# Attention of a hybrid encoder trunk: V becomes the stationary operand, the transposed probabilities move, and two heads share the array's column halves

## What is computed

```python
# A: chunks of 64 queries see their own chunk and the 8 before it
s = jnp.einsum('bnqhd,bnkhd->bnhqk', qc, kb) * (dh ** -0.5)
p = jax.nn.softmax(s + bias, axis=-1)
o = jnp.einsum('bnhqk,bnkhd->bnqhd', p, vb)
oa = o * jax.nn.silu(az)
# C: the same over the 256 best keys of an indexer
p = jax.nn.softmax(jnp.where(sel_ok, s, -jnp.inf), axis=-1)
oc = jnp.einsum('bhqk,bqkhd->bqhd', p, vsel) * jax.nn.silu(cz)
# later: y = sigmoid(ga) * (oa @ w_branch[0]) + ... + sigmoid(gd) * (od @ w_branch[3])
```

## Time and profile before

| | us |
|---|---|
| median of 3 runs (3464.01 to 3467.62) | 3464.07 |
| the profiled execution | 3473.63 |
| its span | 3471.6 |
| TensorE busy in the span | 3128.5 (90%) |
| VectorE, ScalarE, GpSimd busy | 1799.1, 816.6, 668.0 |
| attention C, first layer | about 564 to 692 of the span |
| attention A, first layer | about 1384 to 1511 |
| attention C and A, second layer | about 2284 to 2412, 3103 to 3228 |

### The profile page before, as it was taken

The page is one execution under the profiler, slowest core; times in us unless marked ns, Lnnn a source line. Parts: engine busy times, 40 slices in busy tenths (PEclk is TensorE's granted clock), DMA queues, the critical chain, the costliest instruction groups (busy, mean ns, idle before and its releaser), DMA issues. The chain is left out here.

```text
span 3471.6 us, 45936 instructions
## 1 busy us (share of the span) xinstructions
PE 3128.5 (90%) x18504; PEld 1679.5 (48%) x18504; DVE 1799.1 (52%) x3456; ACT 816.6 (24%) x1542; POOL 668.0 (19%) x476
## 2 busy tenths in 40 slices
PE   7999996899998988899988999968999988898997
PEld 3444443545764446554443534435457544466443
DVE  2179996273334780245112799954722358702542
ACT  2141122431112422410110412234311123324000
POOL 1016331021112313000010163310311122130000
PEclk9999998989999999889999999988999989998998
DMA  5001121010011122054040011200110110210621
GB/s 197 13 15 37 58 79 43 10 42 29 23 41 50 34 69 73 4 183 130 0 140 15 25 37 52 94 25 16 34 47 17 38 49 29 85 54 4 231 81 55
DMA packets 132346, 195.77 MB, mean 56 GB/s; under 512 B 8072, under 2 KB 87976, under 8 KB 131880
## 3 DMA queue, kind: packets, MB, share of 16 engines
q1 hardware_dynamic: 113544, 158.74, 14.1%
q10 hardware_dynamic: 18592, 34.09, 2.7%
HBM read 146.14 MB, written 48.78 MB: 56 GB/s over the span
## 5 line engine op out<-in xcount | busy, mean ns | idle before, releaser
L504 PE MATMUL ps<-hT,wr 128*128 128x512 f32 x1600 | 759.3, 615 | 12.0 <-ACT arena L559 9.2
L504 PEld LDWEIGHTS ps<-hT,wr 128*128 128x128 f32 x1600 | 299.7, 196 | 343.3 <-issue 320.9
L504 PE MATMUL ps<-sums,wr 128*128 128x512 f32 x800 | 395.2, 626 | 13.9 <-ACT gts L569 13.9
L1314 DVE TENSOR_SCALAR_CACHE_REDUCE arena<-arena,sm 128x384 f32<-128x384 f32 (+5 forms) x384 | 337.9, 943 | 2.2
L649 POOL TENSOR_TENSOR gts<-gts,wr 128x512 f32<-128x512 f32 x96 | 132.6, 1381 | 749.7 <-ACT wr L550 494.6
L1032 DVE CUSTOM_DVE_ANT_0 arena<-ps,arena 128x640 f32<-128x640 f32 (+7 forms) x128 | 90.6, 708 | 310.2 <-PE ps L959 249.6
L504 PEld LDWEIGHTS ps<-sums,wr 128*128 128x128 f32 x800 | 151.5, 199 | 178.2 <-issue 155.8
L727 PE MATMUL ps<-xo,arena 128*128 128x512 f32 x512 | 224.0, 600 | 0.9 <-ACT xo L902 0.9
L739 PE MATMUL ps<-wr,hT 128*128 128x512 f32 x512 | 220.1, 592 | 0.0
L504 PE MATMUL ps<-wr 128*128 128x512 f32 x400 | 193.5, 612 | 2.9 <-ACT wr L550 2.9
L989 PEld LDWEIGHTS ps<-arena 128*128 128x128 f32 x1056 | 154.9, 218 | 79.4 <-issue 72.9
(11 more groups left out here) (293 smaller groups left out, 4475.8 us busy)
## 6 DMA issues: line engine op xcount, KB each, us to landing
wr<-in_w_in SPq DMA_DIRECT2D x68, 1024.0 KB, 5.3
gate_tanh<-gts ACTq DMA_DIRECT2D x128, 256.0 KB, 2.0
arena<-gate_tanh SPq DMA_DIRECT2D x128, 256.0 KB, 3.1
x_cur<-arena SPq DMA_DIRECT2D x2, 4096.0 KB, 23.4
arena<-in_w_branch SPq DMA_DIRECT2D x8, 1024.0 KB, 6.5
wr<-in_w_out SPq DMA_DIRECT2D x8, 1024.0 KB, 7.6
arena<-x_cur SPq DMA_DIRECT2D x4, 2048.0 KB, 8.1
arena<-in_x SPq DMA_DIRECT2D x4, 1024.0 KB, 8.1
```

The source lines that it names most:

```text
L504: ins = pe.matmul(ap, lhsT=right(u, w_side)[:, kt, :], rhs=left(h_side, kt), start=fresh and kt == 0, stop=kt == half_k - 1, skip_group_ch ...
L1314: ins = dve.tensor_scalar(compared[i], iscore[i], cbits[:, j:j + 1], None, ALU.is_ge, ALU.add, accum_out=count[:, j:j + 1])
```

## The change

For the values, V is now the stationary operand (128 keys x 64 channels) and the transposed probabilities move (128 columns). The result is transposed already: channels on partitions, queries in columns. Two heads go to the two column halves of the array, that is to partitions 0 to 63 and 64 to 127 of `O`, and are done together at every odd step from `u = 3` on. Even steps hold no values any more. The probabilities get a third buffer. The gate rows `z` are scaled by the reciprocals of the row sums on VectorE (at `u % 4 == 0`), transposed on TensorE in place of the gated output (at `u % 4 == 1`), copied by ScalarE into `xo` as before, and VectorE multiplies them there by `O` (at `u % 4 == 2`). The loop has 34 steps in place of 36, so two steps' fills are done elsewhere. The tail waits for `O` to be emptied where it waited for the ScalarE copy (two lines, in `pe_tail` and `sp_tail`).

```diff
@@ -715,7 +715,7 @@
             pe_fill(pe, KT * len(fills))
             assert fill_at[0] == len(fills) and len(piece_of) == 64 and not todo
-            jobs.stored(pe, ("oT", ORDER[-1], NT - 1))
+            jobs.stored(pe, ("o", ORDER[-1], NT - 1))
             for n, (half, ct, b) in enumerate(tail):
                 key = ("branch", n)
                 if n == 0:
@@ -921,12 +921,12 @@
         MIX = {}
-        def attention(b, q, k, v, z, first_tile, bias, at_s, at_pt, at_og, v_unit=None):
+        def attention(b, q, k, v, z, first_tile, bias, at_s, at_pt, v_unit=None):
             units = [(i, h) for i in range(NT) for h in range(4)]
             rows = [H(at_s), H(at_s + 1)]
-            probs_t = [H(at_pt), H(at_pt + 1)]
-            gated = [H(at_og, 0.25), H(at_og + 0.25, 0.25)]
+            probs_t = [H(a) for a in at_pt]
+            out_t = xo[:, 2 * ORDER.index(b):2 * ORDER.index(b) + 2, :]
             top, neg, tot, rtot = small(2), small(2), small(8), small(8)
             def span(u):
@@ -944,10 +944,10 @@
                 i, h, _, _ = span(u)
                 act_fills(eng, ("values", b, u))
-                if h == 3:
+                if h >= 2:
                     jobs.ready(eng, ("o", b, i))
                 else:
-                    eng.wait_ge(sg("values_" + b), 3 * i + h + 1)
+                    eng.wait_ge(sg("values_" + b), i + 1)
             def scores(pe, u):
@@ -970,39 +970,50 @@
                     ins = pe.transpose(ap[:, P * j:P * j + P], rows[u % 2][:, P * (g + j):P * (g + j) + P], ident)
                 jobs.filled(ins, key)
+            def values(pe, u):
+
+                i, h, k0, nb = span(u)
+                for e in range(2):
+                    jobs.stored(pe, ("PT", b, u + e, groups(nb)[-1][0]))
+                if u == 0 and v_unit is not None:
+                    unit_done(pe, v_unit)
+                o = jobs.open(pe, ("o", b, i), O) if h == 0 else O.ap
+                for j in range(nb):
+                    for e in range(2):
+                        ins = pe.matmul(o[HD * e:HD * e + HD, P * (h // 2):P * (h // 2) + P],
+                                        lhsT=v[:, k0 + j, HD * (h + e):HD * (h + e) + HD],
+                                        rhs=probs_t[(u + e) % 3][:, P * j:P * j + P], start=j == 0, stop=j == nb - 1)
+                for e in range(2):
+                    jobs.mark(("values", b, u + e))
+                if h == 2:
+                    jobs.filled(ins, ("o", b, i))
+                else:
+                    ins.then_inc(sg("values_" + b), 1)
+
             def pe(pe):
-                for u in range(len(units) + 4):
+                for u in range(len(units) + 2):
                     if u < len(units) and u % 2 == 0:
                         scores(pe, u)
...
                         turn(pe, u - 1, groups(span(u - 1)[3])[0])
                     pe_fill(pe, ATT_FILL[b])
-                    if 2 <= u <= len(units) + 1:
-                        i, h, k0, nb = span(u - 2)
-                        jobs.stored(pe, ("PT", b, u - 2, groups(nb)[-1][0]))
-                        if u == 2 and v_unit is not None:
-                            unit_done(pe, v_unit)
-                        if h == 0:
-                            o = jobs.open(pe, ("o", b, i), O)
-                        for j in range(nb):
-                            ins = pe.matmul(o[:, HD * h:HD * h + HD], lhsT=probs_t[u % 2][:, P * j:P * j + P],
-                                            rhs=v[:, k0 + j, HD * h:HD * h + HD], start=j == 0, stop=j == nb - 1)
-                        jobs.mark(("values", b, u - 2))
-                        if h == 3:
-                            jobs.filled(ins, ("o", b, i))
-                        else:
-                            ins.then_inc(sg("values_" + b), 1)
+                    if u >= 3 and u % 2 == 1:
+                        values(pe, u - 3)
                     if 1 <= u <= len(units):
                         for group in groups(span(u - 1)[3])[1:]:
                             turn(pe, u - 1, group)
-                    if u >= 4 and u % 4 == 3:
-                        og = gated[(u // 4 - 1) % 2]
-                        pe_o_turn(pe, b, u // 4 - 1, [og[:, 0:P], og[:, P:2 * P]])
-                assert u % 4 == 3
+                    if u >= 5 and u % 4 == 1:
+                        i = u // 4 - 1
+                        key = ("oT", b, i)
+                        ap = jobs.open(pe, key, T)
+                        pe.wait_ge(sg("z_scaled_" + b), i + 1)
+                        for m in range(2):
+                            ins = pe.transpose(ap[:, P * m:P * m + P], z[:, i, P * m:P * m + P], ident)
+                        jobs.filled(ins, key)
             def act(act):
-                for u in range(len(units) + 4):
+                for u in range(len(units) + 2):
                     if u < len(units):
                         i, h, k0, nb = span(u)
                         act_fills(act, ("S", b, u))
@@ -1012,13 +1023,13 @@
                                        accum_out=tot[:, u % 8:u % 8 + 1]).then_inc(sg("probs_" + b), 1)
                     if 1 <= u <= len(units):
                         i, h, k0, nb = span(u - 1)
-                        if u - 1 >= 2:
-                            wait_values(act, u - 3)
+                        if u - 1 >= 3:
+                            wait_values(act, u - 4)
                         for g, n in groups(nb):
                             ap = act_ready(act, ("PT", b, u - 1, g))
-                            ins = act.activation(probs_t[(u - 1) % 2][:, P * g:P * (g + n)], ap[:, 0:P * n], ACT.Copy)
+                            ins = act.activation(probs_t[(u - 1) % 3][:, P * g:P * (g + n)], ap[:, 0:P * n], ACT.Copy)
                             jobs.emptied(ins, ("PT", b, u - 1, g))
-                    if u >= 4 and u % 4 == 3:
+                    if u >= 5 and u % 4 == 1:
                         act_o_turn(act, b, u // 4 - 1)
             def dve(dve):
@@ -1036,21 +1047,21 @@
                         jobs.stored(dve, ("S", b, u))
                         dve.tensor_scalar(neg[:, u % 2:u % 2 + 1], top[:, u % 2:u % 2 + 1], -1.0, None, ALU.mult)\
                            .then_inc(sg("top_" + b), 1)
+                    if u >= 4 and u % 4 == 0:
+                        i = u // 4 - 1
+                        t4 = 4 * (i % 2)
+                        dve.wait_ge(sg("probs_" + b), u)
+                        link(dve, dve.reciprocal(rtot[:, t4:t4 + 4], tot[:, t4:t4 + 4]))
+                        zh = z[:, i, :].rearrange("p (h d) -> p h d", h=4)
+                        share = rtot[:, t4:t4 + 4].unsqueeze(2).broadcast_to([P, 4, HD])
+                        dve.tensor_tensor(zh, zh, share, ALU.mult).then_inc(sg("z_scaled_" + b), 1)
                     if u >= 6 and u % 4 == 2:
                         i = u // 4 - 1
-                        t4 = 4 * (i % 2)
-                        jobs.ready(dve, ("o", b, i))
-                        link(dve, dve.reciprocal(rtot[:, t4:t4 + 4], tot[:, t4:t4 + 4]))
-                        if i >= 2:
-                            jobs.ready(dve, ("oT", b, i - 2))
-                        o = O.ap
-                        for h in range(4):
-                            cols = slice(HD * h, HD * h + HD)
-                            ins = dve.scalar_tensor_tensor(gated[i % 2][:, cols], o[:, cols], rtot[:, t4 + h:t4 + h + 1],
-                                                           z[:, i, cols], ALU.mult, ALU.mult)
+                        jobs.stored(dve, ("oT", b, i))
+                        ap = jobs.ready(dve, ("o", b, i))
+                        x = out_t[:, :, P * i:P * i + P]
+                        ins = dve.tensor_tensor(x, ap[:, 0:2 * P].rearrange("p (m t) -> p m t", m=2), x, ALU.mult)
                         jobs.emptied(ins, ("o", b, i))
-                        jobs.stored(dve, ("o", b, i))
-                        dve.engine_nop().then_inc(sg("gated_" + b), 1)
             return pe, act, dve
@@ -1065,7 +1076,7 @@
             diagonals = bass.AP(tensor=toep_l.tensor, offset=127, ap=[[768, 4], [-1, P], [1, BAND * P]])
             table = nc.dram_tensor("a_bias_table", [4, P, BAND * P], F32, kind="Internal").ap()
             att = attention("A", q, k, v, z, lambda i: max(0, i - BAND + 1),
-                            lambda i, h, nb: bias8[:, h, P * (BAND - nb):P * BAND], 12, 14, 16, ("A", 1))
+                            lambda i, h, nb: bias8[:, h, P * (BAND - nb):P * BAND], 12, (14, 15, 16), ("A", 1))
             def sp_table(sp, l):
                 sp.dma_start(toep_l, toep[bass.ds(l, 1)].rearrange("l h n -> (l h) n")).then_inc(sg("toep_copied"), 16)
@@ -1131,7 +1142,7 @@
                     return iscore[i]
                 return first_bias[:, 2 * P - P * nb:2 * P]
-            att = attention("C", q, k, v, z, lambda i: 0, bias, 10, 17.25, 12)
```

(1 more changed line is left out.)

2 lines of the change are left out of this document (1 added, 1 removed).

## The result

The changed kernel takes 3489.95 us, median of 7 runs (3481.88 to 3493.68), beside 3467.39 for the kernel before in 7 runs (3459.85 to 3478.2). The ratio is 1.0066, 95% interval 1.0046 to 1.0086: slower, and outside the predicted range of 3438 to 3482. (The prediction counts from 3464.07, the median of the first three of the seven runs before.) Its profiled execution took 3482.95.

What follows compares the result with a forecast made beforehand. Attention C bound by chain scores, VectorE, ScalarE, transposes, TensorE close behind. Per layer C 0.8, A 4.2, fills -1.7: together 3.3, 6.6 in two layers; 3457.5 off the 3464.07 median, said as 3458, range 3438 to 3482.

Steps and rivals of the forecast that it cites:

- Fills: C's last two fills, four records under VectorE's first work for D, move ahead of A: 1.7 us lost per layer.
- Attentions: Attentions C and A, per layer: 0.8 us gained in C, 4.2 in A.
- Even steps, C: Attention C's even steps lose their values; transposes they made late start earlier: 8.0 us gained per layer.
- Changing the tiling: Leaving and refilling around values blocks, about 0.2 us a side: 5.6 lost in C, 1.8 in A with fills, per layer.
- 5.6 + 1.6: Attention C's losses per layer: 5.6 us for tiling changes, 1.6 for one more fall of the clock.
- Overlap of the columns: Two heads' values run fully side by side in column halves: 0.21 us per key tile a pair, 0.43 without overlap.
- The rival without overlap: Columns don't overlap, so odd steps lengthen: 28 us a layer, 56 in all, 3514; chance 8%.
- Late A and the clock: Attention A without fills, steps 14 to 30: 8.5 us a pair instead of 8.8, despite clock falls; 2 us gained per layer.
- 1.5 at the end: End of attention A, last values to the tail's first matmul: a shorter chain and step 32's values gone, 1.5 us less.
- VectorE, "0": Attention's VectorE work: one product replaces four instructions, z scaled earlier; the 24.0 us waits go, counted within the 8.0.
- "Up to twice": Skill's promised speedup for the values: if all were on the path, 56 us less, 3408; chance 2%.
- The chances: Whole kernel's outcome against no change: faster 0.40, same 0.34, slower 0.26.

Runs made afterwards that it cites:

- e1: The changed kernel with the two last attention-loop steps and their fills back, so later fills stand as before the change: 3448.36 us, ratio 0.994 to the kernel before.
- e2: The kernel before without fills in the last two steps of each attention, so later fills stand as in the changed kernel: 3506.85 us, ratio 1.0118.
- e5: The changed kernel with no fills in steps 32 and 33 of attention C either, four fills later than in the kernel before: 3460.1 us, ratio 0.9972.
- e9: The kernel before with unused repeats of the values at five late steps of attention A, where TensorE waits for VectorE: 3448.41 us, ratio 0.9944.
- e8: The kernel before with VectorE's part alone: gate rows scaled early, one product replacing five instructions, probabilities still the weights: 3427.8 us, ratio 0.988.
- e3: e1 with the two value loops exchanged, one head's key tiles after the other's instead of alternating: 3466.54 us, ratio 1.0001 to the kernel before.
- e7: e1 with unused work, one head's values repeated into a free bank at even steps of A from 14 on: 3413.56 us, ratio 0.9851.
- e4: e1 without pairs: V stays the weights, but each step does one head's values: 3427.32 us, ratio 0.9892 to the kernel before.
- e6: The changed kernel with two more fills at the end of D, so later fills stand as in the kernel before: 3471.52 us, ratio 1.0007.

## Why the prediction was wrong, step by step

- **Fills: the step that failed.** The prediction had "4 x 0.43 = 1.7 lost" per layer: the cost of the moved records themselves. Measured: D and B with what lies between them and A took 14.3 and 15.6 us more, 29.9 in two layers against 3.4. e1 and e2 show that the shift alone does it, e5 that it is the phase and not the amount. I had priced four records and not what stands behind them in the one order in which all fills are done; the stages of D and B were never costed, since the diff doesn't touch them. In D the shift makes GpSimd's work on the fills meet VectorE's products at every tile (4.3 us of wait a layer), and TensorE is busy 3.6 us longer at the lower clock; B's part is not explained. The edits moved fills and not GpSimd's work alone, so for D too this last step is read from the traces and not tried.
- **Attentions: right in direction, low in size.** Forecast were 0.8 in C and 4.2 in A, 5.0 a layer. The stages gained 10.9 and 4.2, mean 7.5: C 5.3 and 2.1, A 5.6 and 2.0. C's 5.3 stands in the layer whose stage ahead took 303 us and not 308. Among layers with 303 the old form has 126.7 (e9) and the pairs 123.4 to 124.5, among those with 308 it is 127.9 to 128.8 (once 134.2, in e2) and 126.7 to 128.3; so part of the 5.3 is not the change's. Without the shift e1 is 20 us under the kernel before, where the forecast has 10.
- **Even steps, C: near, partly by luck.** 8.0 was forecast for the even steps. e8, which has the gain of the shorter hold of `O` without the swap, shortens C by 7.7 and 8.5, to 121.0 and 120.4. But 1.7 of the 8.0 were the values of step 32, which e8 keeps, and its clock rose, which the 8.0 did not count.
- **Changing the tiling: about right.** 0.2 a side was taken. Two rows of the changed kernel, attention C, row tile 3, a values block of 16 records and the scores behind it:

```profile
599.24 1.09 PE L983 MATMUL ps<-arena 128*64 128x128 f32 x16
600.26 1.35 PE L959 MATMUL ps<-arena 64*128 64x512 f32 x8
```

  1.02 from start to start, of which 16 records at half of 0.107 are 0.86: 0.16 for the way out. In the pairs form C is 123.4 to 128.3 against e8's 121.0 and 120.4, so swap and pairs cost it some 3 to 7.5; the forecast had 5.6 + 1.6.
- **Overlap of the columns: right** (a block of 1.31 where 1.1 to 1.3 was forecast; e3). The rival without overlap had its price at 28 a layer; e3's C and A together are only 13.9 and 11.5 longer than e1's, so half of it or more was not on the path. The granted clock in e3's late A was 0.88, where e1 had 0.79 and 0.73.
- **Late A and the clock: right on average.** The forecast was a clock of 0.6 to 0.85, and 2 us gained there plus 1.5 at the end. From the scores of step 14 to the tail's first matmul it was 89.1 and 85.6 us before and is 83.9 in both layers: 5.2 and 1.7, mean 3.5. (The 84.00 of the earlier trace rows ends at 1506, not at the tail.) The clock is 0.74 where it was 0.71 and 0.74. What I had not drawn from it is its size: e7 and e9 show that late A pays 8 to 13 us a layer for its falls.
- **VectorE, "0".** I counted the early scaling only as the waits that go. In A it was worth 9 to 13 a layer (e8: 120.1 and 120.2 against 133.0 and 129.5). It is the one part of the change that gained by itself.
- **"Up to twice".** The Trainium skill, page "TensorEngine Tiling (Array Packing)", section "Theoretical Speedup", gives up to twice the speed where a dimension is at most 64. The blocks agree (20 records in 1.31, where ten took 1.22; 91.3 of 153.9 us busy in all); the time does not: e1 is slower than e4 and e8, which have no pairs.
- **The chances.** Added up by their own rule, "same" is 0.35 and "slower" 0.25, where the text has 0.34 and 0.26.

## What to carry to other kernels

Where background work is dealt out in one fixed order, an edit that does two pieces fewer in one place moves all that come after: keep the count, or look at every later stage, and try a shift by a whole piece. When a stage that the diff doesn't touch grows, compare the durations of its instructions and not only the waits: here VectorE's products had become longer beside GpSimd's. Before shortening work on an engine that waits, ask what will stand in the gap; with real work in it A was 8 to 9 us a layer shorter than with the same work spread, and with the gap empty it was longer than in the forms without pairs. Split a change into its parts: VectorE's part alone gave 41 us.

## What the runs showed of the hardware

- Work that no one uses made the kernel faster twice: late A from 78.0 and 81.6 to 68.3 and 68.4 us as the granted clock rose from 0.78 and 0.73 to 1.00 (e7), and A by 7.8 and 7.6 in the kernel before (e9).
- Column halves that share all 128 rows overlap fully: 20 records in 1.31 us alternating, 2.71 in turn.
- VectorE's instructions took longer beside GpSimd's: a product of D's tiles 0.41 us alone and 0.70 to 1.48 beside one, drawn out to 0.28 us after its end (changed kernel, e2, e6).
- The stage ahead of attention C (from the indexer's last product, L1200 or L1211, to the first transpose of C), the same code in all kernels, took either 303 or 308 us, in one layer or the other. In it VectorE searches for the 256 best keys while GpSimd works on fills. The changed kernel has one of each:

```profile
260.40:563.70 303.30, 274.81 (x650) 122.79 (x646) 292.79 (x642) 60.27 (x105) 130.78 (x99) 0.96 0.17 56
1978.60:2286.80 308.20, 273.51 (x650) 122.13 (x646) 297.69 (x642) 60.24 (x105) 130.30 (x99) 0.95 0.17 55
```

  VectorE is busy for 4.9 us more, the whole difference, with the same 642 instructions. The search has 192 short ones, of some 0.17 us. In the layer of 303 us 50 of them are drawn out, to as much as 1.25, in that of 308 us 57, and each of these overlaps an instruction of GpSimd. So the stage falls into one of two patterns of meetings; what chooses between them is not shown. Pairs in C follow it: 123.4 to 124.5 after 303 (six layers), 126.7 to 128.3 after 308 (six). The profiled layers of one and the same program differ in this way, so I do not count a difference of 5 to 9 us a layer in these two stages as a kernel's. The stages of D and B, which mostly repeat within 1 or 2 us, are the better witnesses.
